# A two-layer encoder trunk on one core: the last expert pair's down weights handed over and loaded by column blocks

## The chip, the core and the metric

The kernel runs on one core of a Trainium2 chip. The metric is the device time of the kernel in microseconds (us). A run of another kernel is compared with runs of this one on the same chip.

## The reference, cut to what matters

The trunk has two layers for 256 tokens of width 2048, in float32. Layer 0 mixes tokens with a chunkwise mLSTM, layer 1 with latent attention (MLA). Behind each mixer stands a mixture of experts: 16 experts of inner width 512, two for each token.

```python
def moe_ffn(xn, router_w, router_b, w_gate, w_up, w_down):
    ...
    gates = jnp.sum(jax.nn.one_hot(eidx, N_EXPERTS, dtype=jnp.float32) * w[..., None], axis=1)
    hg = jnp.einsum('td,edf->tef', xt, w_gate)
    hu = jnp.einsum('td,edf->tef', xt, w_up)
    a = jax.nn.silu(hg) * hu * gates[..., None].astype(xt.dtype)
    y = jnp.einsum('tef,efd->td', a, w_down)
```

One expert has three matrices of 4 MB: gate and up (2048 x 512) and down (512 x 2048). So a layer's experts are 192 MB, of which each weight is used once.

## The kernel before

**Units and pairs.** The weights come in units of 1 MB: 128 partitions by 4 contraction steps by 512 columns for gate and up; for down, 128 partitions by one contraction step by all 2048 columns (kept as four blocks of 512). Two experts form a pair and are multiplied side by side, each in one half of TensorE's output partitions. A pair has 24 units, numbered n = 0 to 23: for each half q of the gates and ups the units 8q to 8q + 3 (gate) and 8q + 4 to 8q + 7 (up), then 16 to 23 (down). Eight pairs make the layer: k = 0 to 191 within a layer. The last pair is k = 168 to 191, and its down units are k = 184 to 191.

**Places.** A unit is loaded into one of 18 (and a few more) places in SBUF, two to a double buffer: 0 to 7 are the ring that the mixers also use, 8 and 9 lie in AREA, 10 and 11 over HI, 12 and 13 over the first half of XT_BOTH, 14 and 15 over its second half, 16 and 17 in SPARE. The function seat (L118) says which place a unit gets; for nearly all of a layer it goes round in steps of 18. Before the change the last pair's units 176 to 183 (second half of gates and ups) lie in places 10 to 17, after 158 to 165, and 184 to 191 in places 0 to 7, after 166 to 173.

**Who loads.** All weights go through SP's queue in an order written out by hand (experts, L550). Before a load, SP waits in room (L554) until the unit that held the place is consumed; TensorE counts consumed units in the semaphore unit_used, by the last matmul of each unit (finished, L1159). SP's queue is in order: what waits holds everything behind it. Most of a layer is loaded two units at a time, 2 MB in rows of 16 KB; the last pair is loaded unit by unit, 1 MB in rows of 8 KB (L618 to L621), units 181 and 183 in two halves each with rows of 4 KB (L622 to L629).

**The last four units.** Units 188 to 191 are the second half of the contraction of the pair's down matrices (for both experts). They are not loaded as units but as eight DMAs of 512 KB by column blocks d = 0 to 3, two for each block (L630 to L635). Each takes, for two contraction steps, 512 columns: rows of 2 KB. Both DMAs of a block count on one semaphore, and the function by_columns (L146) gives these places two turns.

**The pair on TensorE.** pair (L1156) multiplies gates and ups into banks 0 and 1 (L1183), scatters the pair before in between, turns the activation (L1203) and its selection (L1206, L1208), and multiplies with the down weights into banks 4 to 7. A float32 matmul is two records in the profile. For a normal pair, and for the first two of the four contraction steps c of the last pair, the loop is over c outside and over the column blocks d inside (L1226). For c = 2 and 3 of the last pair the loop over d is outside: it waits for the two DMAs of block d, does 8 matmul records (L1239), tells ScalarE that the block is done, and scatters block d - 1 (L1126, L1127). In layer 0, turn_final (L1062), which turns the first finished columns for the next mixer, stands between the last block's matmuls and the scatter of block 2. Then comes scatter_last (L1130).

**Behind a block.** ScalarE copies and rounds block d (Y_hi, L1660), VectorE makes the low part (Y_lo, L2272), TensorE scatters both to tokens, and VectorE adds them to X (add_block, L2254). The additions of blocks 0 and 1 stand after the low parts of blocks 1 and 2, those of blocks 2 and 3 after the low part of block 3. In layer 1 the blocks of X are stored as they are final (L713, L716 and one store on ScalarE's queue).

**Behind layer 0.** The MLA mixer's weights come through the ring, places 0 to 7; each load waits for the last expert unit that held its place (unit, L510). ScalarE makes the high part of each unit (high, L1463), VectorE the low part (L1842). The turned tokens get their high part from ScalarE (final_high, L1632) and their low part from GpSimd (L742). TensorE multiplies in three passes (L804): high weights by high tokens, low weights by high tokens, and, for the first units last, high weights by low tokens.

Of the kernel before, what the change touches and what calls it, by code (L numbers as in the profile page):

```python
# [18 lines left out]
P = 128  # L19
# [5 lines left out]
UNIT_K = 4  # L25
# [70 lines left out]
BY_COLUMNS = PAIRS * PAIR_UNITS - 4  # L96
# [16 lines left out]
def in_turn(k):  # L113

    return k // 4 * 4 + (0, 2, 1, 3)[k % 4]


def seat(k):  # L118


    if k == ALONE:
        return WIDE + ONCE
    if k == WIDE + ONCE:
        return ALONE
    if EARLY <= k < EARLY + ALONE:
        return k - EARLY
    return k if k < WIDE - 2 else k + 2 if k < WIDE else k - 2 if k < WIDE + 2 else k if k < EARLY else (k - ONCE) % WIDE
# [7 lines left out]
def expert(u):  # L135

    return U_MOE0 <= u < U_CKV or u >= U_MOE1


def split(u):  # L140

    k, singles = (u - U_MOE0, SINGLES[0]) if u < U_CKV else (u - U_MOE1, SINGLES[1])
    return expert(u) and (k in singles or PAIRS * PAIR_UNITS - HALVES <= k < BY_COLUMNS)


def by_columns(u):  # L146

    return expert(u) and (u - U_MOE0 if u < U_CKV else u - U_MOE1) >= BY_COLUMNS


def places():

    slots, turns, held = [], [], [0] * EARLY

    for u in range(U_ALL):
        if u < U_MOE0:
            s = u % RING
        elif u < U_CKV:
            s = seat(u - U_MOE0)
        elif u < U_MOE1:  # L160
            s = (u - U_CKV) % RING
        else:
            k = seat(u - U_MOE1)
            s = (k + U_MOE1 - U_CKV) % RING if k < RING else k
        if by_columns(u):
            held[s] += 2
        elif not expert(u) or s % 2 == 0 or split(u):
            held[s] += 1
        slots.append(s)
        turns.append(held[s])  # L170
    return slots, turns
# [67 lines left out]
def trunk(nc, w, out):  # L239
# [8 lines left out]
    with ctx:  # L248
# [258 lines left out]
        def _(sp):  # L507
# [42 lines left out]
            def experts(layer, base):  # L550
# [67 lines left out]
                for k in sorted(range(PAIRS * PAIR_UNITS - HALVES, BY_COLUMNS), key=in_turn):  # L618
                    room(k, 1)
                    if k - front not in LAST_UPS:  # L620
# [9 lines left out]
                room(BY_COLUMNS, 4)  # L630
                for d in range(4):
                    for k in (BY_COLUMNS, BY_COLUMNS + 2):
                        sp.dma_start(DOUBLE[PLACE[base + k]][:, :, d, :],
                                     all_of[k // 2].rearrange("p (k b c) -> p k b c", k=2, b=4)[:, :, d, :])\
                            .then_inc(sem(f"unit_loaded_{PLACE[base + BY_COLUMNS + d]}"), 16)  # L635

# [133 lines left out]
        def _(pe):  # L770
# [296 lines left out]
            def experts(l, base):  # L1067
# [88 lines left out]
                def pair(m, j, g, following, arrived, slot, consumed, whole, prev, first=False, opened=False, late=False):  # L1156
# [60 lines left out]
                    last_one = whole and not following  # L1217
                    for c in range(FC // 2 if last_one else FC):
# [15 lines left out]
                    for d in range(4 if last_one else 0):  # L1234
                        unit_arrived(pe, base + BY_COLUMNS + d)
                        for c in range(FC // 2, FC):
                            for e in range(2):
                                n = 16 + 4 * (c // 2) + 2 * e + c % 2
                                last = pe.matmul(PS[64 * e:64 * e + 64, 4 + d, :], m_["AT"][:, c, 64 * e:64 * e + 64],  # L1239
                                                 slot(n)[:, d, :], start=False, stop=(c == FC - 1))  # L1240
                                if d == 3:
                                    finished(last, n)
                        if d < 3:
                            last.then_inc(sem(m + "y_done"), 1)
                        if d == 3 and l == 0:
                            turn_final(0)
                        if d:
                            scatter(m, j, d - 1, True)
# [1341 lines left out]

# [13 lines left out]
```

## Time and profile before

| | us |
|---|---|
| median of 3 runs | 1668.2 (1666.77 to 1669.68) |
| the profiled execution | 1667.65 |
| its span, first to last instruction | 1665.6 |
| TensorE busy with matmuls | 1613.5 (97%) |
| VectorE busy | 763.7 (46%) |
| ScalarE busy | 481.3 (29%) |
| bytes moved by the DMA engines | 533.74 MB, mean 320 GB/s |

Times of an event are counted from the span's start. A row of the timeline has the start, the duration, the engine, the line of the kernel, the operation, what it writes and reads, and how many like it were merged; in square brackets the idle time ahead of it and what ended it. Matmuls are pipelined, so the duration of one is longer than the step from it to the next. A row of SP's queue is the issue of a DMA, not its transfer.

### The profile page before, as it was taken

Reading aid. Unit: us, or ns where it says so; the run is one execution under the profiler, and the core shown is the slowest. Engines: PE = TensorE matmul, PEld = TensorE weight load, DVE = VectorE, ACT = ScalarE, POOL = GpSimd, SP = SyncE. Lnnn points to the kernel's source line nnn. Section 1 sums busy time; section 2 is a strip of 40 time slices with the busy share of each in tenths; the row PEclk is TensorE's granted clock in tenths of the full one; section 3 lists DMA queues with packets and bytes.
Section 4 is the critical chain, followed back from the end, with each engine's and each line's share of the span. In section 5 each row is a group of like instructions: output and inputs, shape, how many; then the busy total and the mean of one; then the engine's idle time right before and its main releaser. Section 6 shows DMA issues by size and latency. Waiting matters only on the chain.

```text
span 1665.6 us, 19483 instructions
## 1 busy us (share of the span) xinstructions
PE 1613.5 (97%) x8047; PEld 1013.9 (61%) x8047; DVE 763.7 (46%) x1310; ACT 481.3 (29%) x620; POOL 54.1 (3%) x32
## 2 busy tenths in 40 slices
PE   9999999999999999988999999999999999989997
PEld 7888888887433434333359999888753344334343
DVE  6885477754332222212257777784532323222222
ACT  6445456443100000000054566564320000000000
POOL 3000000000000000000030000020000000000000
PEclk9999999999999999999999999999999999999999
DMA  8765656477999999999995545554799999999998
GB/s 293 266 201 161 200 153 220 151 257 303 422 415 421 429 427 427 428 427 426 420 352 174 159 139 151 197 178 152 287 422 421 424 428 428 427 428 428 429 420 327
DMA packets 117809, 533.74 MB, mean 320 GB/s; under 512 B 13108, under 2 KB 32088, under 8 KB 86488
## 3 DMA queue, kind: packets, MB, share of 16 engines
q1 hardware_dynamic: 117200, 532.06, 81.8%
q8 instruction: 66, 1.08, 0.3%
q10 hardware_dynamic: 488, 0.40, 0.1%
q14 instruction: 23, 0.19, 0.0%
q0 software_dynamic: 32, 0.02, 0.0%
HBM read 530.33 MB, written 2.11 MB: 320 GB/s over the span
## 4 chain that ended last, share of the span: by engine, by line
PE 81%; DMA 15%; DVE 1%; SPq 1%; ACT 1%; issue 0%; DVEq 0%; ACTq 0%
PE PS L804 33%; PE PS L1183 21%; PE PS L1226 8%; DMA DOUBLE<-in_moe_w_down 4%; DMA SPARE<-in_moe_w_gate 4%; DMA OVD<-in_moe_w_gate 3%; PE PS L915 3%; DMA OVD<-in_moe_w_down 2%; PE PS L1089 2%; DMA WIDED<-in_moe_w_gate 2%; PE PS L1126 2%; PE PS L936 1%; PE PS L921 1%; PE PS L1127 1%; PE PS L1109 1%; PE PS L1014 1%
## 5 line engine op out<-in xcount | busy, mean ns | idle before, releaser
L1842 DVE TENSOR_TENSOR LO<-ring,HI 128x2048 fp32r<-128x2048 f32 (+1 forms) x124 | 267.1, 2154 | 164.1 <-ACT HI L1463 163.5
L1183 PE MATMUL PS<-DOUBLE,AREA 128*64 128x512 f32 x1136 | 309.3, 598 | 8.8 <-DMA OVD<-in_moe_w_gate 5.4
L1463 ACT ACTIVATE HI<-ring 128x2048 fp32r<-128x2048 f32 (+1 forms) x124 | 223.6, 1803 | 260.4 <-PE PS L804 233.8
L804 PE MATMUL PS<-HI,XT_BOTH 128*128 128x512 f32 (+1 forms) x1344 | 297.9, 373 | 0.6 <-issue 0.6
L804 PEld LDWEIGHTS PS<-HI,XT_BOTH 128*128 128x128 f32 x1344 | 243.9, 188 | 35.0 <-issue 1.9
L1183 PE MATMUL PS<-OVD,AREA 128*64 128x512 f32 x464 | 209.5, 602 | 3.5 <-DMA SPARE<-in_moe_w_up 2.7
L1183 PEld LDWEIGHTS PS<-DOUBLE,AREA 128*64 128x64 f32 x1136 | 98.1, 139 | 177.8 <-issue 177.5
L1226 PE MATMUL PS<-DOUBLE,AREA 128*64 128x512 f32 x592 | 156.3, 595 | 8.0 <-DMA DOUBLE<-in_moe_w_down 7.6
L2264 DVE TENSOR_TENSOR AREA<-PS,VFF 128x512 f32<-128x512 f32 x64 | 44.1, 689 | 238.1 <-PE PS L1089 204.8
L804 PE MATMUL PS<-LO,XT_BOTH 128*128 128x512 f32 (+1 forms) x672 | 152.5, 368 | 0.0
L1650 ACT ACTIVATE AREA<-PS 128x512 f32<-128x512 f32 x16 | 9.6, 597 | 439.4 <-PE PS L1183 439.4
L804 PEld LDWEIGHTS PS<-LO,XT_BOTH 128*128 128x128 f32 x672 | 122.9, 188 | 16.2
L2254 DVE TENSOR_TENSOR X<-PS,X 128x512 f32<-128x512 f32 x112 | 69.9, 682 | 121.2 <-PE PS L1127 121.2
L1660 ACT ACTIVATE Y_hi<-PS,AREA 128x512 fp32r<-128x512 f32 x64 | 44.0, 687 | 230.2 <-PE PS L1226 195.3
L1183 PEld LDWEIGHTS PS<-OVD,AREA 128*64 128x64 f32 x464 | 63.0, 140 | 65.0 <-issue 65.0
L1226 PEld LDWEIGHTS PS<-DOUBLE,AREA 128*64 128x64 f32 x592 | 50.3, 137 | 81.8 <-issue 77.1
L2272 DVE SCALAR_TENSOR_TENSOR Y_lo<-PS,AREA,Y_hi 128x512 fp32r<-128x512 f32 x64 | 48.0, 751 | 107.9 <-ACT Y_hi L1660 103.1
L1183 PE MATMUL PS<-SPARE,AREA 128*64 128x512 f32 x208 | 92.5, 594 | 0.0
L1183 PE MATMUL PS<-WIDED,AREA 128*64 128x512 f32 x192 | 86.8, 596 | 0.0
L1089 PEld LDWEIGHTS PS<-AREA,XN 128*128 128x128 f32 x448 | 47.9, 140 | 34.0 <-issue 34.0
L1226 PE MATMUL PS<-OVD,AREA 128*64 128x512 f32 x144 | 63.9, 595 | 3.4 <-DMA WIDED<-in_moe_w_down 3.4
L1089 PE MATMUL PS<-AREA,XN 128*128 128x128 f32 x448 | 61.2, 280 | 0.0
(331 smaller groups left out, 1843.8 us busy)
## 6 DMA issues: line engine op xcount, KB each, us to landing
DOUBLE<-in_moe_w_up SPq DMA_DIRECT2D x26, 2048.0 KB, 24.4
ring<-in_a_w_in SPq DMA_DIRECT2D x48, 1024.0 KB, 5.2
DOUBLE<-in_moe_w_gate SPq DMA_DIRECT2D x24, 2048.0 KB, 21.4
DOUBLE<-in_moe_w_down SPq DMA_DIRECT2D x24, 2048.0 KB, 28.6
DOUBLE<-in_moe_w_down SPq DMA_DIRECT2D x26, 1024.0 KB, 9.0
ring<-in_b_w_in SPq DMA_DIRECT2D x32, 768.0 KB, 4.5
DOUBLE<-in_moe_w_gate SPq DMA_DIRECT2D x22, 1024.0 KB, 11.5
DOUBLE<-in_moe_w_up SPq DMA_DIRECT2D x20, 1024.0 KB, 14.0
```

The lines of the kernel that those rows point to most:

```text
L804: mm = pe.matmul(PS[:, banks[t], 0:n], lhs(k0 + kk, t)[part], weights[:, kk, 0:n], start=first and kk == 0 and p == 0, stop=last and kk == ...
L915: pe.matmul(PS[:, 4 * (b % 2) + ch, :], HI[u % 2][:, kk, ch * P:(ch + 1) * P], XT_BOTH[:, :, k, :], start=k == 0, stop=False)
L1089: last = pe.transpose(PS[:, GATHER_BANKS[g] + k // 2, at_:at_ + P], XN[:, t, c * P:(c + 1) * P], m_["SEL"][:, t, :])
L1126: pe.matmul(PS[:, bank, :], SCT[:, t * P:(t + 1) * P], YH[:, d, :], start=True, stop=False)
L1183: last = pe.matmul(PS[64 * e:64 * e + 64, up, :], tokens_of(c, e), slot(units[e])[:, kk, :], start=(c == 0), stop=(c == DC - 1))
L1226: last = pe.matmul(PS[64 * e:64 * e + 64, 4 + d, :], m_["AT"][:, c, 64 * e:64 * e + 64], slot(units[e])[:, d, :], start=(c == 0), stop=(c ...
L1463: act.activation(HI[s % 2][:, :, 0:n], ring[PLACE[u]][:, :, 0:n], ACT.Copy).then_inc(sem("hi_ready"), 1)
L1660: act.activation(YH[:, d, :], PS[:, 4 + d, :], ACT.Copy, scale=m_["GS"])\
L1842: tt(LO[PLACE[u]][:, :, 0:n], ring[PLACE[u]][:, :, 0:n], HI[s % 2][:, :, 0:n], ALU.subtract)\
L2254: tt(xs, PS[:, bank, :], xs, ALU.add).then_inc(sem(counted), 1)
L2264: tt(m_["XG"][:, 4 * g:4 * g + 4, :].rearrange("p k (t s) -> p k t s", t=NT), PS[:, banks[g]:banks[g] + 2, :].rearrange("p b (k t s) -> p ...
L2272: stt(YL[:, d, :], PS[:, 4 + d, :], m_["GS"], YH[:, d, :], ALU.mult, ALU.subtract)\
```

## The change

The host hands over one more input, last_down, which holds the down matrices of each layer's last pair again, cut as [layer, expert, block d, 128 partitions, 4 contraction steps x 512 columns]. Each of the eight down units 184 to 191 of the last pair is now one such piece: unit 184 + 2d + e is block d of expert e with all four contraction steps, 1 MB that is contiguous in memory, in rows of 8 KB, loaded by one DMA with a semaphore and a turn of its own. by_columns and its double turns are gone.

The places of the last pair's second half are exchanged: 176 to 183 go to places 0 to 7, and 184 to 191 to places 10 to 17. Units from 184 on are consumed in the order of their numbers (in_turn).

On TensorE the last pair's down matmuls are all done by blocks in a new function: for each d it waits for both units, does the four contraction steps (16 matmul records), and scatters block d - 1 after the second of them.

```diff
-BY_COLUMNS = PAIRS * PAIR_UNITS - 4
+BY_COLUMNS = PAIRS * PAIR_UNITS - 8
@@ def in_turn(k):
-    return k // 4 * 4 + (0, 2, 1, 3)[k % 4]
+    return k if k >= BY_COLUMNS else k // 4 * 4 + (0, 2, 1, 3)[k % 4]
@@ def seat(k):
+    if k >= BY_COLUMNS:
+        return k - BY_COLUMNS + RING + 2
+    if k >= BY_COLUMNS - RING:
+        return k - BY_COLUMNS + RING
@@ experts, on SP
-                for k in sorted(range(PAIRS * PAIR_UNITS - HALVES, BY_COLUMNS), key=in_turn):
+                for k in sorted(range(PAIRS * PAIR_UNITS - HALVES, PAIRS * PAIR_UNITS), key=in_turn):
                     room(k, 1)
-                    if k - front not in LAST_UPS:
+                    if k >= BY_COLUMNS:
+                        d, e = divmod(k - BY_COLUMNS, 2)
+                        sp.dma_start(in_double(base + k).rearrange("p k c -> p (k c)"), w["last_down"][layer, e, d])\
+                            .then_inc(sem(f"unit_loaded_{PLACE[base + k]}"), 16)
+                    elif k - front not in LAST_UPS:
...
-                room(BY_COLUMNS, 4)
-                for d in range(4):
-                    for k in (BY_COLUMNS, BY_COLUMNS + 2):
-                        sp.dma_start(DOUBLE[PLACE[base + k]][:, :, d, :],
-                                     all_of[k // 2].rearrange("p (k b c) -> p k b c", k=2, b=4)[:, :, d, :])\
-                            .then_inc(sem(f"unit_loaded_{PLACE[base + BY_COLUMNS + d]}"), 16)
@@ pair, on TensorE
-                    last_one = whole and not following
-                    for c in range(FC // 2 if last_one else FC):
+                    if whole and not following:
+                        down_by_columns(m, j, slot, finished)
+                        return
+                    for c in range(FC):
...
+                def down_by_columns(m, j, slot, finished):
+                    for d in range(4):
+                        for e in range(2):
+                            unit_arrived(pe, base + BY_COLUMNS + 2 * d + e)
+                        if d == 2:
+                            pe.wait_ge(sem(m + "sct_ready"), j + 1)
+                        for c in range(FC):
                             for e in range(2):
-                                n = 16 + 4 * (c // 2) + 2 * e + c % 2
+                                n = BY_COLUMNS - (PAIRS - 1) * PAIR_UNITS + 2 * d + e
                                 last = pe.matmul(PS[64 * e:64 * e + 64, 4 + d, :], m_["AT"][:, c, 64 * e:64 * e + 64],
-                                                 slot(n)[:, d, :], start=False, stop=(c == FC - 1))
-                                if d == 3:
+                                                 slot(n)[:, c, :], start=(c == 0), stop=(c == FC - 1))
+                                if d and c == e == 0:
+                                    finished(last, n - 1)
+                                if c == FC - 1 and (e == 0 or d == 3):
                                     finished(last, n)
+                            if c == 1 and d:
+                                scatter(m, j, d - 1, True)
                         if d < 3:
                             last.then_inc(sem(m + "y_done"), 1)
                         if d == 3 and l == 0:
                             turn_final(0)
-                        if d:
-                            scatter(m, j, d - 1, True)
@@ on the host
+def down_blocks(inputs):
+    import numpy as np
+    pair = [PER_GRP * (2 + e) + PER_GRP - 1 for e in range(2)]
+    a = np.asarray(inputs["moe_w_down"])[:, pair].reshape(2, 2, 2, P, 2, 4, UNIT_C)
+    return np.ascontiguousarray(a.transpose(0, 1, 5, 3, 2, 4, 6).reshape(2, 2, 4, P, UNIT_K * UNIT_C))
```

## Rows read from the trace of the kernel before

**Rows 1.** The page: busy time, granted clock in 40 slices, issues with us to landing.

```profile
PE 1613.5 (97%) x8047; PEld 1013.9 (61%) x8047; DVE 763.7 (46%) x1310; ACT 481.3 (29%) x620; POOL 54.1 (3%) x32
...
PEclk9999999999999999999999999999999999999999
...
ring<-in_a_w_in SPq DMA_DIRECT2D x48, 1024.0 KB, 5.2
```

**Rows 2.** Windows: from:to, length, then the columns that the first row names.

```profile
core 0: us, PE busy (x) PEld busy (x) DVE busy (x) ACT busy (x) POOL busy (x), PEclk, DMA share, GB/s
...
881.00:1100.00 219.00, 219.00 (x1235) 203.64 (x1234) 158.50 (x317) 125.80 (x187) 0.00 (x0) 1.00 0.52 164
...
1614.00:1624.00 10.00, 9.85 (x46) 3.82 (x45) 3.40 (x6) 0.00 (x0) 0.00 (x0) 1.00 1.01 419
...
1644.00:1650.00 6.00, 5.00 (x26) 1.78 (x23) 0.30 (x1) 0.69 (x1) 0.00 (x0) 1.00 1.04 382
```

**Rows 3.** Timeline of SP's queue in layer 1: units 176, 184 to 187, the columns.

```profile
1587.50 4.31 SPq L563 DMA_DIRECT2D OVD<-in_moe_w_gate  x1
...
1613.88 10.43 SPq L563 DMA_DIRECT2D DOUBLE<-in_moe_w_down  x4
1624.35 19.84 SPq L633 DMA_DIRECT2D DOUBLE<-in_moe_w_down  x8
```

**Rows 4.** Timeline of TensorE: matmuls of units 173 and 175, of 180 and 182.

```profile
1615.14 3.66 PE L1183 MATMUL PS<-DOUBLE,AREA 128*64 128x512 f32 x16
...
1628.50 0.62 PE L1183 MATMUL PS<-OVD,AREA 128*64 128x512 f32 x1 [1.33 <-DMA SPARE<-in_moe_w_up]
```

**Rows 5.** Timeline of TensorE: layer 1's last pair, down matmuls.

```profile
1638.58 3.65 PE L1226 MATMUL PS<-DOUBLE,AREA 128*64 128x512 f32 x16 [0.75 <-DMA DOUBLE<-in_moe_w_down]
1643.57 3.65 PE L1226 MATMUL PS<-DOUBLE,AREA 128*64 128x512 f32 x16 [1.33 <-DMA DOUBLE<-in_moe_w_down]
...
1649.94 1.94 PE L1239 MATMUL PS<-DOUBLE,AREA 128*64 128x512 f32 x8 [1.00 <-DMA DOUBLE<-in_moe_w_down]
...
1655.92 1.94 PE L1239 MATMUL PS<-DOUBLE,AREA 128*64 128x512 f32 x8
```

**Rows 6.** Timeline of SP's queue: unit 187 and the last column DMA, both layers.

```profile
818.17 2.13 SPq L563 DMA_DIRECT2D DOUBLE<-in_moe_w_down  x1
...
839.45 1.82 SPq L633 DMA_DIRECT2D DOUBLE<-in_moe_w_down  x1
...
1622.19 2.12 SPq L563 DMA_DIRECT2D DOUBLE<-in_moe_w_down  x1
...
1643.01 1.19 SPq L633 DMA_DIRECT2D DOUBLE<-in_moe_w_down  x1
```

**Rows 7.** DMA issues of 1613.88, 1622.19, 1643.01, 818.17, 839.45: KB, us to landing.

```profile
DOUBLE<-in_moe_w_down SPq DMA_DIRECT2D x1, 1024.0 KB, 22.1
...
DOUBLE<-in_moe_w_down SPq DMA_DIRECT2D x1, 1024.0 KB, 21.2
...
DOUBLE<-in_moe_w_down SPq DMA_DIRECT2D x1, 512.0 KB, 12.1
...
DOUBLE<-in_moe_w_down SPq DMA_DIRECT2D x1, 1024.0 KB, 21.9
...
DOUBLE<-in_moe_w_down SPq DMA_DIRECT2D x1, 512.0 KB, 12.0
```

**Rows 8.** Timeline of TensorE in layer 0: last block, first unit's third pass.

```profile
852.03 1.94 PE L1239 MATMUL PS<-DOUBLE,AREA 128*64 128x512 f32 x8
...
861.43 2.07 PE L804 MATMUL PS<-HI,XT_BOTH 128*128 128x512 f32 x8
```

**Rows 9.** Timelines of ScalarE and GpSimd in layer 0, behind the last block.

```profile
854.04 0.69 ACT L1660 ACTIVATE Y_hi<-PS,AREA 128x512 fp32r<-128x512 f32 x1 [2.33 <-PE PS L1239]
...
856.43 1.14 ACT L1632 ACTIVATE XT_BOTH<-AREA 128x512 fp32r<-128x512 f32 x2
...
857.13 8.95 POOL L742 TENSOR_TENSOR XT_BOTH<-AREA,XT_BOTH 128x512 fp32r<-128x512 f32 x4 [518.26 <-ACT XT_BOTH L1632]
```

More of the change, by code:

```diff
@@ L142, in split @@
     k, singles = (u - U_MOE0, SINGLES[0]) if u < U_CKV else (u - U_MOE1, SINGLES[1])
-    return expert(u) and (k in singles or PAIRS * PAIR_UNITS - HALVES <= k < BY_COLUMNS)
-def by_columns(u):
-    return expert(u) and (u - U_MOE0 if u < U_CKV else u - U_MOE1) >= BY_COLUMNS
+    return expert(u) and (k in singles or k >= PAIRS * PAIR_UNITS - HALVES)
 def places():
@@ L164, in places @@
             s = (k + U_MOE1 - U_CKV) % RING if k < RING else k
-        if by_columns(u):
-            held[s] += 2
-        elif not expert(u) or s % 2 == 0 or split(u):
+        if not expert(u) or s % 2 == 0 or split(u):
             held[s] += 1
@@ L1233, in pair @@
                             gather(m, following, (1,))
-                    for d in range(4 if last_one else 0):
-                        unit_arrived(pe, base + BY_COLUMNS + d)
-                        for c in range(FC // 2, FC):
+                def down_by_columns(m, j, slot, finished):
[5 more added lines that the diff above has]
+                        for c in range(FC):
                             for e in range(2):
-                                n = 16 + 4 * (c // 2) + 2 * e + c % 2
+                                n = BY_COLUMNS - (PAIRS - 1) * PAIR_UNITS + 2 * d + e
                                 last = pe.matmul(PS[64 * e:64 * e + 64, 4 + d, :], m_["AT"][:, c, 64 * e:64 * e + 64],
-                                                 slot(n)[:, d, :], start=False, stop=(c == FC - 1))
-                                if d == 3:
+                                                 slot(n)[:, c, :], start=(c == 0), stop=(c == FC - 1))
+                                if d and c == e == 0:
+                                    finished(last, n - 1)
+                                if c == FC - 1 and (e == 0 or d == 3):
                                     finished(last, n)
+                            if c == 1 and d:
+                                scatter(m, j, d - 1, True)
                         if d < 3:
@@ L2598 @@
     arrays["in_consts"] = constants()
+    arrays["in_last_down"] = down_blocks(inputs)
     w = {n[3:]: nc.dram_tensor(n, a.shape, mybir.dt.float32, kind="ExternalInput").ap() for n, a in arrays.items()}
```

## The prediction

> **What bounds the kernel now.** I read the page first. TensorE is busy for 97% of the span and its granted clock stays in the top tenth, the 2.4 GHz level, throughout [rows 1]. The busy share alone does not say who sets the end, so I went stage by stage with the table of windows. In the latent-attention mixer, from 881 to 1100 us, TensorE is busy for all 219 us while the DMA engines are half idle: TensorE is the bound. In the experts, 1614 to 1624 us, the DMA engines are full at 419 GB/s [rows 2], and TensorE waits for weights again and again [rows 4, 5]: the load stream is the bound. The change touches both places where these stages meet something else: the end of layer 0's experts, where TensorE takes over, and the end of layer 1's, which is the end of the kernel. So I then read the timeline of SP's queue, TensorE's timeline around the last pair, and the issues with their time to landing. I price three things: when the last down weights land, how much TensorE has to do after that, and whether the new buffer order starves the stream.
>
> **When the weights land.** Units 184 to 187 are 1 MB in rows of 8 KB per partition. In layer 1 the first is issued at 1613.88 [rows 3] and lands 22.1 us later, at 1635.98; the fourth is issued at 1622.19 [rows 6] and lands 21.2 us later, at 1643.39 [rows 7]: 7.41 us for three, 2.47 us a unit. The window's 419 GB/s gives 1.049 MB / 419 GB/s = 2.50 us [rows 2]. I take 2.49. The eight column DMAs of 512 KB that follow read rows of 2 KB. The last is issued at 1643.01 [rows 6] and lands 12.1 us later, at 1655.1 [rows 7]: 11.7 us for 4 MB, 2.93 us per MB, and the stretch shows 382 GB/s [rows 2]. After the change these 4 MB are four more units with 8 KB rows: 1643.4 + 4 x 2.49 = 1653.35, so the last landing moves 1.75 us forward. Layer 0 in the same way: 818.17 + 21.9 = 840.07 [rows 6, 7]; the last column DMA lands at 839.45 + 12.0 = 851.45 [rows 6, 7]; after, 840.07 + 9.96 = 850.0, 1.4 us forward.
>
> **What TensorE does after the last landing.** Before, a block d needs only the second half of the contraction, 8 matmul records, and then scatters the block before it. From the first step after a wait, 1649.94, to the start of the last block, 1655.92, there are two such steps [rows 5], so one is 2.99 us; the last 8 records take 1.94 us and end at 1657.86 [rows 5]. TensorE is already 0.8 us behind the last landing there. After, a block holds all four contraction steps: 16 records and, between them, the scatter of the block before: 2.99 + 1.94 = 4.93 us. Blocks 0 and 1 use exactly the four units that arrived first before as well. Block 0 starts at 1638.58 as before and takes 3.65 us, block 1 waits until 1643.57 as before [rows 5]. Then the DMA's 2 x 2.49 = 4.98 us a block is just over TensorE's 4.93: block 2 starts near 1648.5, and block 3 waits for 1653.35 + 0.1 (the usual 0.05 to 0.15 from landing to start, 1643.39 to 1643.57 in these rows) = 1653.45 and ends at 1658.4. Against 1657.86 that is **+0.5 us**. The 1.75 us that the stream wins are spent because the last block carries 16 records and a scatter behind its landing, not 8. What follows, the copy, the low part, the additions of blocks 2 and 3 and the stores, has the same order on ScalarE and VectorE, so I carry it over unchanged. Moving scatter 2 ahead of the end saves nothing there: it lay beside ScalarE's 0.7 us copy and VectorE's low part anyway.
> Bounds: if all weights were there in time, TensorE alone would need two blocks without a gap, where the second 8 records cost 3.65 - 1.94 = 1.71 us [rows 5], and a last one: 1643.57 + 2 x 4.70 + 4.93 = 1657.9, so not below +0.05. From above, a stream at the 382 GB/s of its last stretch would land the last unit at 1643.4 + 4 x 2.74 = 1654.4 and end at 1659.4, +1.5.
>
> **Layer 0.** The last block ends at 852.03 + 1.94 = 853.97 now [rows 8]. After: 850.0 + 0.1 + 4.93 = 855.05, which is +1.1. Here scatter 2 comes before this end, and before it stood after it, so TensorE by itself would be back to about +0.1. But who waits for that end is ScalarE: its copy starts at 854.04, right behind; then the high part of the first mixer unit, the high part of the turned tokens at 856.43, and then GpSimd's low parts from 857.13, 2.24 us each (four in 8.95) [rows 9], two of them until 861.6. TensorE's third pass over the first unit starts at 861.43 [rows 8], at that very moment: this chain has no slack. It moves by the full **+1.1 us**, TensorE idles in front of it, and from there TensorE is the bound without a gap [rows 2], so nothing gives it back and layer 1 starts later by the same amount. Bounds: +0.1 if that chain has slack that I don't see, and +2.1 at 2.74 us a unit.
>
> **Waits and buffers.** The change swaps places. Units 176 to 183, the last pair's second gates and ups, now take the places of 166 to 173 instead of 158 to 165, so SP must wait longer before it issues them, and everything behind waits with it in SP's queue, the down units too. Now 176 is issued at 1587.50 [rows 3]. After, the last of them, 183, waits for unit 173, whose matmuls run from 1615.14 to 1618.8 [rows 4]. The stream doesn't feel this as long as it has work: TensorE waits for 182 until 1628.5 [rows 4], so at 1618.8 the engines still hold almost 10 us of loads. The 12 DMAs behind (four halves, eight down units) go out at 2.6 us each if SP is as slow as in its 10.43 us for four [rows 3]: the last by 1650.1, and the engines need it at 1650.9. I cost the longer wait at nothing; its cover is those 10 us of queued loads. The down units themselves wait for 158 to 165, free long before. The other side of the swap: places 0 to 7 are free earlier at layer 0's end, so the mixer's units 4 to 7 can be issued earlier. Nobody waits for them: TensorE has no gap on a DMA there [rows 2]. Instruction counts stay: the same matmuls, one more semaphore wait a block, eight issues for eight.
>
> **A rule weighed.** The rows say that row length matters here: 2.93 us per MB with rows of 2 KB, 2.49 with 8 KB [rows 2, 3, 6, 7]. The Trainium skill (DMA: Bandwidth & Descriptors, Specifications) puts the minimum for line rate at 512 B, by which 2 KB rows would be at line rate already and the last landing would stay where it is; this trace does not agree, and what would follow is my second rival. The same page (Anatomy of one DMA) fits a DMA as 2.0 us plus its bytes at 436 GB/s; taken one after another, eight of 512 KB would need 25.6 us and four of 1 MB 17.6. The rows have 11.7 us for the eight, so behind a filled queue the fixed part is hidden.
>
> **Sum.** +1.1 and +0.5 make +1.6 us. The profiled execution took 1667.65 us with a span of 1665.6; after, 1669.25. The three runs' median is 1668.2, 0.55 above the profiled one, so I predict 1669.8.
>
> **The rivals.**
> *The landing decides (faster).* If the last blocks followed the landing with the same delay as now, the 1.4 and 1.75 us would come through: 1668.2 - 3.15 = 1665.05. For it: TensorE does wait for DMAs up to 1649.94. Against: from there to the end it doesn't, and the last block gets twice its matmuls. Chance 0.07.
> *No earlier landing (slower).* The last unit lands at 851.45 and 1655.1 as before, be it that row length isn't what slows the last stretch but the end of the stream itself. Then 851.5 + 4.93 = 856.4 (+2.45) and 1655.15 + 4.93 = 1660.1 (+2.2): 1672.85. Against: it would have to come from the end of the stream, yet layer 0 has more loads queued behind and needs 11.4 us for its 4 MB too. Chance 0.10.
> *The stream runs dry (slower).* Place: SP's wait for unit 173. It decides once TensorE releases 173 less than an issue-to-landing time before the queue is empty; the 1 MB loads of the first mixer, with a short queue, take 5.2 us [rows 1], so from about 1623 on, 4 us later than I compute. It could come sooner if a thin queue runs slower. Price: each us dry is a us, in each layer; with 3 us each, 1669.8 + 6 = 1675.8. Chance 0.08.
> *Another placement of the tensors in memory*, now 16.8 MB more, changes the rate of all loads by a tenth of a per cent or two either way: no row prices it. Chance 0.05.
>
> **How the numbers follow.** The forecast has 0.70: +0.2 to +3.6 by the bounds above, so 1668.4 to 1671.8, and with the runs' scatter of 1.5 either way 1667 to 1673. The range 1666.8 to 1673.2 takes in the second rival too and leaves out the first and the third. A kernel like this can be told from no change by about 0.2%, 3.3 us. Faster by more: half of the first rival and some of the last, 0.06. Slower by more: the second and third, and the forecast's upper edge, 0.20. Within: 0.74.
>
> **What would show it.** Right: the down units of the last pair land 2.5 us apart up to about 1653.4 (plus layer 0's shift of 1.1); TensorE's blocks of 16 records start at their landings; the last block ends some 5 us after the last landing; in layer 0 a new idle gap of about 0.9 us before the mixer's first matmuls. Wrong: a DMA rate below 400 GB/s between 1618 and 1650, a TensorE wait for an up unit longer than now, landings 2.9 us apart, or a block that takes much more than 4.9 us.

## The result, and the profile after

The kernel before took 1668.2 us (median of 13 runs), the changed one 1672.3 us (13 runs, 1670.0 to 1673.1). The ratio is 1.0022, 95% interval 1.0015 to 1.0029, so the change costs 3.7 us (2.5 to 4.8); the two medians are 4.1 us apart. The forecast was 1669.8 within 1666.8 to 1673.2: the range and the sign are right, the size is 2.5 us short (+1.6 forecast, +4.1 by the medians). The profiled execution of the changed kernel took 1672.57 us.

The page first. TensorE's busy time is 0.2 us from that of [rows 1], its instructions are as many, and its clock is at the same level. TensorE does the same work and waits 5 us longer.

```profile
span 1670.6 us, 19479 instructions
...
PE 1613.7 (97%) x8047; PEld 1014.0 (61%) x8047; DVE 763.5 (46%) x1310; ACT 481.1 (29%) x620; POOL 54.1 (3%) x32
...
PEclk9999999999999999999999999999999999999999
```

The windows of the changed kernel answer to [rows 2]. The columns are from:to, length, then as the first row names them.

```profile
core 0: us, PE busy (x) PEld busy (x) DVE busy (x) ACT busy (x) POOL busy (x), PEclk, DMA share, GB/s
1616.00:1626.00 10.00, 10.00 (x46) 4.13 (x43) 2.48 (x4) 0.00 (x0) 0.00 (x0) 1.00 1.01 421
1626.00:1636.00 10.00, 8.50 (x39) 3.27 (x39) 1.98 (x3) 0.60 (x1) 0.00 (x0) 1.00 1.02 415
1646.00:1652.00 6.00, 4.93 (x20) 1.73 (x20) 0.75 (x1) 0.40 (x2) 0.00 (x0) 1.00 1.00 414
...
881.00:1100.00 219.00, 219.00 (x1228) 203.09 (x1227) 158.74 (x318) 124.02 (x184) 0.00 (x0) 1.00 0.52 165
```

The stretch near the end, 382 GB/s in [rows 2], is at 414 now, so the longer rows do load faster. The mixer, 881 to 1100, is as full as it was.

SP's queue in layer 1 answers to [rows 3] and [rows 6]. A row is the start, the time that the issues took, the line, and what is written from what. L628 are the halves of units 181 and 183, L619 the new down units.

```profile
1600.69 10.59 SPq L560 DMA_DIRECT2D DOUBLE<-in_moe_w_gate  x4
...
1622.16 1.75 SPq L628 DMA_DIRECT2D DOUBLE<-in_moe_w_up  x4
1623.96 0.91 SPq L619 DMA_DIRECT2D OVD<-in_last_down  x2
1624.91 2.09 SPq L619 DMA_DIRECT2D WIDED<-in_last_down  x2
1627.05 2.60 SPq L619 DMA_DIRECT2D OVD<-in_last_down  x2
1629.69 3.40 SPq L619 DMA_DIRECT2D SPARE<-in_last_down  x2
```

Unit 176 goes out at 1600.69, where [rows 3] have 1587.50. That is the longer wait for places. The twelve issues behind it take 10.9 us in all.

TensorE in layer 0, the changed kernel's timeline, answers to [rows 8]. L1241 are the down matmuls, L1120 a scatter's first matmul, L770 turn_final, L798 the mixer's matmuls (L804 before).

```profile
837.14 3.65 PE L1241 MATMUL PS<-OVD,AREA 128*64 128x512 f32 x16 [0.70 <-DMA OVD<-in_last_down]
842.11 1.94 PE L1241 MATMUL PS<-WIDED,AREA 128*64 128x512 f32 x8 [1.32 <-DMA WIDED<-in_last_down]
...
852.04 1.94 PE L1241 MATMUL PS<-SPARE,AREA 128*64 128x512 f32 x8
853.91 0.50 PE L1120 MATMUL PS<-Y_hi,SCT 128*128 128x512 f32 x1
...
855.05 1.94 PE L1241 MATMUL PS<-SPARE,AREA 128*64 128x512 f32 x8
856.92 1.09 PE L770 MATMUL PS<-CON,X 128*128 128x128 f32 x8
...
860.73 2.06 PE L798 MATMUL PS<-HI,XT_BOTH 128*128 128x512 f32 x8 [0.54 <-ACT XT_BOTH L1636]
...
864.44 2.09 PE L798 MATMUL PS<-HI,XT_BOTH 128*128 128x512 f32 x8
```

The last block ends at 855.05 + 1.94 = 856.99, 3.02 us later than in [rows 8], and the third pass starts at 864.44, 3.01 later. ScalarE and GpSimd, which answer to [rows 9], carry the same 3.02 us:

```profile
857.06 0.69 ACT L1664 ACTIVATE Y_hi<-PS,AREA 128x512 fp32r<-128x512 f32 x1 [4.35 <-PE PS L1241]
...
859.45 1.14 ACT L1636 ACTIVATE XT_BOTH<-AREA 128x512 fp32r<-128x512 f32 x2
```

```profile
860.15 8.94 POOL L736 TENSOR_TENSOR XT_BOTH<-AREA,XT_BOTH 128x512 fp32r<-128x512 f32 x4 [521.02 <-ACT XT_BOTH L1636]
```

TensorE in layer 1, the changed kernel's timeline, answers to [rows 5]:

```profile
1641.87 3.65 PE L1241 MATMUL PS<-OVD,AREA 128*64 128x512 f32 x16 [0.73 <-DMA OVD<-in_last_down]
1646.85 1.94 PE L1241 MATMUL PS<-WIDED,AREA 128*64 128x512 f32 x8 [1.32 <-DMA WIDED<-in_last_down]
...
1652.73 1.94 PE L1241 MATMUL PS<-OVD,AREA 128*64 128x512 f32 x8 [0.95 <-issue]
...
1657.72 1.94 PE L1241 MATMUL PS<-SPARE,AREA 128*64 128x512 f32 x8
...
1660.71 1.94 PE L1241 MATMUL PS<-SPARE,AREA 128*64 128x512 f32 x8
```

Block 2, due at once, waits 0.95 us. The timeline names "issue", yet the second of its two units landed at 1628.63 + 24.0 = 1652.6, by this row of the DMA issues (KB, us to landing):

```profile
OVD<-in_last_down SPq DMA_DIRECT2D x1, 1024.0 KB, 24.0
```

The eight units land at 1639.25, 1641.73, 1644.22, 1646.71, 1649.20, 1652.64, 1655.11 and 1657.58: 2.48 us apart but for one step of 3.44. In layer 0 all steps are 2.48 to 2.50, from 834.52 to 851.91.

### The profile page after: what moved, and what is told of

Its sections match the earlier page's. It is cut to its first block, busy times and chain, and to the rows that moved or that the text cites. A ratio compares the mean times of both kernels' runs of the same rounds, so it can differ in the third digit from the quotient of the medians.

```text
span 1670.6 us, 19479 instructions
## 1 busy us (share of the span) xinstructions
PE 1613.7 (97%) x8047; PEld 1014.0 (61%) x8047; DVE 763.5 (46%) x1310; ACT 481.1 (29%) x620; POOL 54.1 (3%) x32
## 4 chain that ended last, share of the span: by engine, by line
PE 81%; DMA 16%; DVE 2%; ACT 1%; issue 0%; SPq 0%; DVEq 0%; ACTq 0%
PE PS L798 33%; PE PS L1177 20%; PE PS L1222 8%; DMA DOUBLE<-in_moe_w_down 5%; DMA DOUBLE<-in_moe_w_gate 4%; DMA SPARE<-in_moe_w_gate 4%; PE PS L909 3%; DMA WIDED<-in_last_down 3%; PE PS L1083 2%; PE PS L1120 2%; PE PS L930 1%; PE PS L915 1%; PE PS L1241 1%; PE PS L1121 1%; PE PS L1103 1%; PE PS L1008 1%
## 5 line engine op out<-in xcount | busy, mean ns | idle before, releaser
L1177 PE MATMUL PS<-DOUBLE,AREA 128*64 128x512 f32 x1264 | 334.3, 595 | 10.6 <-DMA OVD<-in_moe_w_gate 5.4
L798 PE MATMUL PS<-HI,XT_BOTH 128*128 128x512 f32 (+1 forms) x1344 | 297.9, 373 | 1.1 <-issue 0.6
L798 PEld LDWEIGHTS PS<-HI,XT_BOTH 128*128 128x128 f32 x1344 | 243.9, 188 | 35.5 <-issue 2.4
L1177 PEld LDWEIGHTS PS<-DOUBLE,AREA 128*64 128x64 f32 x1264 | 107.2, 138 | 194.4 <-issue 194.1
L1177 PE MATMUL PS<-OVD,AREA 128*64 128x512 f32 x400 | 177.7, 595 | 0.4 <-DMA SPARE<-in_moe_w_up 0.4
L798 PE MATMUL PS<-LO,XT_BOTH 128*128 128x512 f32 (+1 forms) x672 | 152.5, 368 | 0.0
L1222 PE MATMUL PS<-DOUBLE,AREA 128*64 128x512 f32 x528 | 141.7, 595 | 4.2 <-DMA DOUBLE<-in_moe_w_down 3.8
L798 PEld LDWEIGHTS PS<-LO,XT_BOTH 128*128 128x128 f32 x672 | 122.9, 188 | 16.2
L1222 PEld LDWEIGHTS PS<-DOUBLE,AREA 128*64 128x64 f32 x528 | 45.7, 137 | 69.5 <-issue 66.2
L1177 PEld LDWEIGHTS PS<-OVD,AREA 128*64 128x64 f32 x400 | 53.8, 138 | 44.4 <-issue 44.4
L1177 PE MATMUL PS<-SPARE,AREA 128*64 128x512 f32 x176 | 78.5, 594 | 1.0 <-DMA DOUBLE<-in_moe_w_gate 1.0
L1177 PE MATMUL PS<-WIDED,AREA 128*64 128x512 f32 x160 | 72.2, 596 | 1.6 <-DMA OVD<-in_moe_w_up 1.6
L1222 PE MATMUL PS<-OVD,AREA 128*64 128x512 f32 x144 | 63.9, 595 | 3.4 <-DMA WIDED<-in_moe_w_down 3.4
```

Of the source, the lines that this page charges most:

```text
L798: mm = pe.matmul(PS[:, banks[t], 0:n], lhs(k0 + kk, t)[part], weights[:, kk, 0:n], start=first and kk == 0 and p == 0, stop=last and kk == ...
L1177: last = pe.matmul(PS[64 * e:64 * e + 64, up, :], tokens_of(c, e), slot(units[e])[:, kk, :], start=(c == 0), stop=(c == DC - 1))
```

## The experiments

Theory A, that of the prediction: the last landing comes forward, but the last block now has 16 matmul records and a scatter behind its landing, and this costs more. Rival B: the second copy of the weights in memory, or its place, is what costs. Rival C: the exchange of places costs, through SP's later issues. Rival D: rows of 8 KB bring nothing. Beside them stood the question which part of the last block could be spared.

The table cuts each profiled execution at the same events: the landing of unit 187 (the fourth down unit), the end of the last down block on TensorE, and the span's end. All are us. The last column is the median beside the kernel before on the same chip, as a ratio with its 95% interval.

| kernel | 187 lands, layer 0 | to block end | to landing, layer 1 | to block end | to span end | ratio |
|---|---|---|---|---|---|---|
| before | 840.09 | 13.88 | 789.46 | 14.43 | 7.7 | |
| changed | 841.97 | 15.02 | 789.72 | 15.94 | 7.9 | 1.0022 [1.0015, 1.0029] |
| changed, again | 842.76 | 15.11 | 789.97 | 15.73 | 7.9 | 1.0020 [1.0011, 1.0029] |
| places as before | 841.82 | 15.02 | 789.90 | 15.72 | 7.9 | 1.0018 [1.0009, 1.0027] |
| scatter 2 behind | 841.70 | 13.72 | 789.56 | 14.94 | 7.7 | 1.0010 [1.0001, 1.0019] |
| half blocks, 8 KB | 840.03 | 13.23 | 789.34 | 14.22 | 7.7 | 0.9997 [0.9988, 1.0006] |
| handed over only | 840.52 | 13.41 | 790.39 | 13.36 | 7.9 | 1.0002 [0.9993, 1.0011] |
| whole blocks, 2 KB | 842.74 | 16.10 | 790.66 | 16.45 | 7.9 | 1.0035 [1.0021, 1.0049] |
| before, longer start | 849.52 | 13.35 | 791.00 | 13.29 | 7.9 | 1.0063 [1.0049, 1.0077] |
| changed, longer start | 850.77 | 15.03 | 790.60 | 14.82 | 7.9 | 1.0075 [1.0061, 1.0088] |

Columns two to five hold what the change does near its place; the first holds what an execution had gathered before it reached the changed part.

**Handed over only.** The kernel before, with the last pair's down weights read from a second tensor of the same size as the change's, in the same rows and the same order.

```diff
-                        single(base + k, all_of[k // 2])
+                        single(base + k, all_of[k // 2] if k < BY_COLUMNS - 4 else w["last_down"][layer, k // 2 % 2, 0])
...
-                                     all_of[k // 2].rearrange("p (k b c) -> p k b c", k=2, b=4)[:, :, d, :])\
+                                     w["last_down"][layer, k // 2 % 2, 1].rearrange("p (k b c) -> p k b c", k=2, b=4)[:, :, d, :])\
```

> The kernel before, with one thing changed: the last pair's down matrices come from a second tensor of 16.8 MB that the host hands over, cut as before (the same row lengths, the same DMAs, the same order). In the two profiles the changed kernel is 1.9 us later than before already at unit 187 of layer 0, ahead of everything that the change touches on TensorE. Theory A (that offset is the scatter of single executions, and the change costs where TensorE and the stream meet): no difference, -0.8 to +0.8 us against the kernel before. Rival B (the extra tensor places the weights differently in memory and the loads run slower): +1.5 to +2.5 us, and the landings drift apart in the expert stages.

Measured: 1667.54 us against 1668.22. Rival B falls: another 16.8 MB in memory and reading from it cost nothing that can be told (by the interval at most 1.8 us). (In the table its 13.36 is short and its 790.39 long because unit 187 itself was late, 3.09 us after the one before.)

**Scatter 2 behind the last block.** The changed kernel; the scatter of block 2 no longer stands in the middle of block 3 but behind it.

```diff
-                            if c == 1 and d:
+                            if c == 1 and d in (1, 2):
                                 scatter(m, j, d - 1, True)
...
                             turn_final(0)
+                        if d == 3:
+                            scatter(m, j, 2, True)
```

> The changed kernel, but the scatter of block 2 stands behind the last block's matmuls (in layer 0 behind turn_final too), as in the kernel before, not in their middle. Theory A (what sets the end is the chain that begins when the last block's matmuls end: ScalarE's copy and what hangs on it, in both layers): the last block ends 1.0 us earlier behind the same landing, in layer 0 and in layer 1, so 2.0 us less than the changed kernel, or +1.5 to +2.5 us against the kernel before. My prediction said that this scatter's place saves nothing in layer 1 (it costs nothing beside ScalarE's copy), without seeing that it costs its 1.0 us where it stands now. Rival B (placement) and rival C (the exchange of places starves the stream): no difference to the changed kernel, about +4.1 us against the kernel before.

Measured: 1669.18 us, 3.2 us below the changed kernel's 1672.33 (2.0 us by their two ratios), and 1.0 us above the kernel before. TensorE's timeline of this kernel in layer 0:

```profile
851.77 3.65 PE L1241 MATMUL PS<-SPARE,AREA 128*64 128x512 f32 x16
855.36 1.09 PE L770 MATMUL PS<-CON,X 128*128 128x128 f32 x8
856.21 0.47 PE L1120 MATMUL PS<-Y_hi,SCT 128*128 128x512 f32 x1
...
859.14 2.06 PE L798 MATMUL PS<-HI,XT_BOTH 128*128 128x512 f32 x8
```

and in layer 1:

```profile
1651.30 1.94 PE L1241 MATMUL PS<-OVD,AREA 128*64 128x512 f32 x8 [1.23 <-issue]
...
1656.27 3.65 PE L1241 MATMUL PS<-SPARE,AREA 128*64 128x512 f32 x16
```

The last block is one row of 16 records of 3.65 us, not 4.93 in three pieces. From the landing of 187 to its end is 1.3 us less in layer 0 and 1.0 less in layer 1, and the mixer's first matmuls (859.14) have no gap before them. The scatter itself then fills time in which TensorE would have waited for ScalarE: from the block's end to the mixer's first row are 859.14 - 855.42 = 3.72 us with it and 860.73 - 856.99 = 3.74 without it. So over half of what the change costs is this one scatter, standing where ScalarE's chain waits for the block.

**Half blocks in 8 KB rows.** The kernel before; only contraction steps 2 and 3 are handed over, four units of 1 MB with block d of both experts, in rows of 8 KB. Steps 0 and 1, the last block of 8 records and the scatter behind it stay.

```diff
-                for k in sorted(range(PAIRS * PAIR_UNITS - HALVES, BY_COLUMNS), key=in_turn):
+                for k in sorted(range(PAIRS * PAIR_UNITS - HALVES, PAIRS * PAIR_UNITS), key=in_turn):
                     room(k, 1)
+                    if k >= BY_COLUMNS:
+                        sp.dma_start(in_double(base + k).rearrange("p k c -> p (k c)"), w["last_down"][layer, k - BY_COLUMNS])\
...
-                                n = 16 + 4 * (c // 2) + 2 * e + c % 2
                                 last = pe.matmul(PS[64 * e:64 * e + 64, 4 + d, :], m_["AT"][:, c, 64 * e:64 * e + 64],
-                                                 slot(n)[:, d, :], start=False, stop=(c == FC - 1))
+                                                 slot(20 + d)[:, 2 * e + c % 2, :], start=False, stop=(c == FC - 1))
```

> The kernel before with only the row length changed: units 184 to 187 and all of TensorE's order as before, but the second half of the contraction is handed over as four units of 1 MB, one for each column block d with both experts and both contraction steps, in rows of 8 KB, one DMA each in place of two with rows of 2 KB. Places as before. Theory A: the last landing comes 1.7 us earlier, but TensorE, which needs 3.46 us for c = 1 and then 1.9 + 3.0 + 3.0 + 1.9 us, has the end from the landing of unit 187 on: the last block ends 1.0 us earlier in layer 1 (its wait of 1.0 us goes) and 0.4 us earlier in layer 0, together -1.4 us against the kernel before (-0.5 to -2.5). Rival B: the same gain less 1.5 to 2 us for placement, so about +0.3. Rival D (row length isn't what slowed the stream's end): 2 KB or 8 KB, the landings stay 2.7 to 2.9 us per MB apart, and no difference.

Measured: 1667.69 us, not to be told from the kernel before; the profiled execution is 1.1 us shorter in its span. The last landing is early, 850.03 where the kernel before has 851.41, and still the block's end gains only 0.65 us in layer 0 and 0.2 in layer 1. Beside the handed-over kernel, whose landings behind unit 187 are even, it gains 0.2 in layer 0 too (13.23 against 13.41). TensorE's timeline of this kernel in layer 0 says why:

```profile
840.16 3.65 PE L1216 MATMUL PS<-DOUBLE,AREA 128*64 128x512 f32 x16 [1.31 <-DMA DOUBLE<-in_moe_w_down]
843.62 3.63 PE L1228 MATMUL PS<-DOUBLE,AREA 128*64 128x512 f32 x16
847.18 0.50 PE L1116 MATMUL PS<-Y_hi,SCT 128*128 128x512 f32 x1
...
851.32 1.94 PE L1228 MATMUL PS<-DOUBLE,AREA 128*64 128x512 f32 x8
```

After its last wait at 840.16 TensorE has no gap to 853.26. From there TensorE, not the landing, is the bound, and 13.2 us is what its work takes in this order. In layer 1 it does wait once:

```profile
1648.90 1.94 PE L1228 MATMUL PS<-DOUBLE,AREA 128*64 128x512 f32 x8 [0.80 <-DMA DOUBLE<-in_last_down]
```

This is a late landing of the changed kernel's kind: 1645.10, then 1648.86, 3.76 us apart.

**Places as before.** The changed kernel with the old order of places.

```diff
-    if k >= BY_COLUMNS:
-        return k - BY_COLUMNS + RING + 2
-    if k >= BY_COLUMNS - RING:
-        return k - BY_COLUMNS + RING
```

> The changed kernel without the exchange of places: units 176 to 183 again in places 10 to 17 behind 158 to 165, the down units 184 to 191 in places 0 to 7 behind 166 to 173. Theory A: SP issues units 176 to 183 some 13 us earlier and nothing else moves, because the engines had 10 us of loads queued all the time: no difference to the changed kernel, about +4.1 us against the kernel before (+3.3 to +4.9). Rival C (the later issue costs, by a thinner queue or by SP's waits): 1 us or more less than the changed kernel.

Measured: 1671.59 us, ratio 1.0018 beside 1.0022 and 1.0020 of the changed kernel, so the same. SP's queue in layer 1 issues the halves up to 15 us earlier than the changed kernel:

```profile
1606.93 2.08 SPq L624 DMA_DIRECT2D OVD<-in_moe_w_up  x1
...
1617.79 15.36 SPq L615 DMA_DIRECT2D DOUBLE<-in_last_down  x8
```

and the fourth down unit lands at 1646.74, in the changed kernel at 1646.71. Rival C falls: the stream was full either way.

**Changed, again.** The changed kernel unaltered, for a second profile and a second median.

> The changed kernel itself, once more. Theory A and every rival: about +4 us against the kernel before (+3 to +5). Its profile is read for two things that one execution can't tell: whether the 1.5 us that the loads are behind before the changed part begins are there again, and whether the step of 3.4 us in place of 2.5 between two landings of layer 1's down units is there again, beside a fetch of 16 KB of instructions.

Measured: 1671.33 us. The table's columns two to five agree with the first profile within 0.25 us each. The late landing is there again at the same unit (1650.34 to 1653.73, 3.39 us), and block 2 waits 0.91 us. The loads are late ahead of the changed part again, but in another way: 2.5 us already at the first expert load, which lands at 265 us in the kernel before, and 2.7 us at the landing of 822 us.

**The same blocks in rows of 2 KB.** The changed kernel; each down unit is read from the original matrices by two DMAs of 512 KB.

```diff
-                        sp.dma_start(in_double(base + k).rearrange("p k c -> p (k c)"), w["last_down"][layer, e, d])\
-                            .then_inc(sem(f"unit_loaded_{PLACE[base + k]}"), 16)
+                        for c in range(2):
+                            sp.dma_start(in_double(base + k)[:, 2 * c:2 * c + 2, :],
+                                         all_of[(BY_COLUMNS + 4 * c + 2 * e) // 2].rearrange("p (k b c) -> p k b c", k=2, b=4)[:, :, d, :])\
+                                .then_inc(sem(f"unit_loaded_{PLACE[base + k]}"), 16)
```

> The changed kernel with the row length put back: the same units, places, order and matmuls, but each down unit is loaded from the original down matrices by two DMAs of 512 KB in rows of 2 KB. Theory A (row length sets how far apart they land: 2.73 us per MB by the 382 GB/s of the column DMAs, against 2.49): unit 187 lands 1.0 us later and the last 1.9 us later than in the changed kernel; 5.46 us a block is then longer than TensorE's 4.93, so the last block ends 1.9 us later in each layer: +3.8 us against the changed kernel, about +7.8 us against the kernel before. Rival D (row length doesn't matter, the end of the stream was slow for another reason): no difference to the changed kernel, about +4 us.

Measured: 1673.82 us, ratio 1.0035 [1.0021, 1.0049], so 2.5 us above the changed kernel beside it. The sign is right, the size smaller than the 3.8 us expected. Windows of this kernel, with the columns as above:

```profile
1634.00:1644.00 10.00, 8.90 (x44) 3.96 (x40) 2.90 (x6) 0.60 (x1) 0.00 (x0) 1.00 1.04 392
1644.00:1654.00 10.00, 8.02 (x36) 2.99 (x36) 0.75 (x1) 0.69 (x1) 0.00 (x0) 1.00 1.05 387
```

and TensorE's last block in layer 1:

```profile
1661.02 1.94 PE L1245 MATMUL PS<-SPARE,AREA 128*64 128x512 f32 x8 [1.09 <-DMA SPARE<-in_moe_w_down]
...
1664.01 1.94 PE L1245 MATMUL PS<-SPARE,AREA 128*64 128x512 f32 x8
```

The whole of 8 MB goes at 387 to 392 GB/s; every other DMA lands 2.7 us after the one before (in layer 1 1647.31, 1650.01, 1652.73, 1655.43, 1658.02). That is 0.2 us more for each MB than with 8 KB rows, as expected (2.73 against 2.49). Rival D falls too, and in layer 1 last block and landing now stand as Theory A says: 1660.88 lands, 1661.02 starts, 1665.95 ends, 4.93 us. The DMAs are also half as large here, but size isn't it: the 512 KB halves of units 181 and 183, in rows of 4 KB, land 1.27 us apart in the changed kernel (1634.22, 1635.48, 1636.75), 2.5 us for each MB. The short rows also lie apart in memory, where the handed-over pieces are contiguous; these two weren't separated.

Why the median moved by 2.5 us and not 3.8 isn't shown. In the profiles the local cost is larger: from the last landing ahead of the down units to the end of the last block are 28.40 and 27.30 us, in the changed kernel 24.96 and 25.90. In layer 1 there is no late landing here, which saves 1 us. In layer 0 there is one, unit 187 at 842.74, 4.16 us after the unit before it. TensorE idles 3.23 us for it, and behind this wait the granted clock is 0.57 between 843 and 847 us, so mostly at the 1.2 GHz level: the first 8 records take 3.20 us and not 1.94. The timeline's row, and the window with its columns as above:

```profile
842.88 3.20 PE L1245 MATMUL PS<-WIDED,AREA 128*64 128x512 f32 x8 [3.23 <-DMA WIDED<-in_moe_w_down]
```

```profile
843.00:847.00 4.00, 4.00 (x11) 1.44 (x11) 0.00 (x0) 0.00 (x0) 0.00 (x0) 0.57 1.06 389
```

This execution was also the slowest of its five (1675.82).

**Both kernels with a longer start.** An attempt to move the instruction fetches against the stream: 32 small matmuls at the start in place of two wide ones, once in the kernel before, once in the changed one.

```diff
-            fill(512, 512)
+            fill(*(32 for _ in range(32)))
```

> The kernel before, with 120 instructions more on TensorE in its first 5 us: its two filling matmuls of 512 columns are 32 of 32 columns, which take about as long and compute nothing that is used. So each fetch of 16 KB of TensorE's instructions behind comes at another point of the work, by roughly half a block. Theory E (a fetch holds one DMA engine for 1.1 us, and the stream loses that where it comes at a bad moment; where it comes is an accident of the program's length): the time moves by 0.5 to 2 us either way against the kernel before, and the landing that is late in layer 1 (1649.9) is another one or none. Rival F (the fetches cost the same wherever they are): -0.5 to +0.5 us, and the same landings.

> The changed kernel with the same 120 instructions more at the start. Theory E: the offset of 1.5 us ahead of the changed part and the late landing in layer 1 (0.95 us) are accidents of where the fetches come; one or both go or change, and the time moves by up to 2.5 us, rather down than up, to between +1.5 and +4.5 us against the kernel before. Rival G (both belong to the change): +3.5 to +4.5 us as the changed kernel.

Measured: 1678.06 and 1680.96 us, both some 10 us above what they should be. Neither range expected against the kernel before holds, and as a test of the fetches this was a poor one. The row of the small matmuls, in the kernel before so altered, where the two wide ones took 3.78 us:

```profile
1.59 13.87 PE L869 MATMUL PS<-AREA 128*128 128x32 f32 x64 [1.59 <-DVE AREA L1831]
```

What it does give: with all of the kernel later by the same 10 us, the changed kernel is still 2.9 us slower than the one before (1679.4 to 1681.2 against 1677.1 to 1678.9). And in the changed kernel the late landing has moved from unit 189 to unit 187 (1652.92 to 1656.40, 3.48 us), where TensorE waits 2.32 us for it and not the usual 1.32:

```profile
1656.53 1.94 PE L1241 MATMUL PS<-WIDED,AREA 128*64 128x512 f32 x8 [2.32 <-DMA WIDED<-in_last_down]
...
1669.28 1.94 PE L1241 MATMUL PS<-SPARE,AREA 128*64 128x512 f32 x8
```

From that landing to the block's end are then 14.82 us, 0.15 below the 14.97 of the prediction, since no further landing is late. In the kernel before with the longer start it is unit 187 too that lands late (1650.03 to 1653.87, 3.84 us):

```profile
1654.00 3.65 PE L1226 MATMUL PS<-DOUBLE,AREA 128*64 128x512 f32 x16 [2.67 <-DMA DOUBLE<-in_moe_w_down]
...
1665.22 1.94 PE L1239 MATMUL PS<-DOUBLE,AREA 128*64 128x512 f32 x8
```

From it to the block's end are 13.29 us. So this pair compares the two orders behind even landings: +1.5 us in layer 1, and +1.7 in layer 0 (15.03 against 13.35).

## Why the prediction was right or wrong

**When the weights land: right in layer 0, one step off in layer 1.** From unit 187 to the last landing are 851.91 - 841.97 = 9.94 us in layer 0; the prediction had 4 x 2.49 = 9.96. In layer 1 it is 10.87.

**What TensorE does after it: right.** 16 records and a scatter take 4.95 us in layer 0 (852.04 to 856.99 with no gap) and 4.93 in layer 1, TensorE keeps up with two units of 2.49 and no more, and from a landing of 187 to the end of the last block layer 0 takes 15.02 us; the prediction had 855.05 - 840.07 = 14.98, that is +1.1.

**Layer 0's +1.1: right beside this profile, and passed on in full.** ScalarE's copy, the high part, GpSimd and the third pass are all 3.01 to 3.03 us later, the 1.9 us of the first column and these 1.1. The mixer gave nothing back (789.7 to layer 1's landing, against 789.5). The gap before the mixer's first matmuls is 0.54 us, where 0.9 was said. But the size is partly luck. In the profile of the kernel before, the first column is complete 3.19 us after unit 187 (840.09 to 843.28), and TensorE waits 0.44 us at 846.03. In the handed-over kernel that step is 2.71 us, TensorE doesn't wait, and the block ends after 13.41 us, not 13.88; with the longer start after 13.35. Against these the change costs 1.6 to 1.7 us in layer 0.

**Layer 1's +0.5: the term that was mis-sized.** It measured +1.5 (15.94 against 14.43), and +1.3 the second time. The failed step is "block 3 waits for 1653.35 + 0.1", which spaced the four landings evenly. One of them was 0.95 us late, and in the new order block 2 waits for it at once and all behind it has no slack: 0.5 + 0.95. The kernel before has a late landing too. Its four columns are complete 2.71 us apart in layer 0 (843.28, 845.99, 848.70, 851.41), but in layer 1 at 1646.13, 1649.90, 1652.50 and 1655.06, with one step of 3.77. I read its effect, the 1.00 us of idle at 1649.94 in [rows 5], as the stream's pace, and took 2.93 us for each MB as the mean over it. At 2.71 that column is complete at 1648.84, TensorE doesn't wait, and the kernel before ends its last block 1.0 us earlier. So I set an uneven stream before against an even one after; both with a late landing, as they ran, are 1.5 us apart, and so are the two with the longer start, even behind unit 187 (14.82 against 13.29).

**Scatter 2: rightly counted, wrongly judged.** The 4.93 us contained it, and the sum came out. But the sentence that moving it ahead "saves nothing there" looked only at where it had been. Where it went, it stands on the path of every block's end: the scatter behind the block takes 1.3 and 1.0 us back. Without it the change's local cost is -0.2 us in layer 0 and +0.5 in layer 1, beside the profile of the kernel before.

**Waits and buffers at nothing: right.** Places as before gives the same time. The pace of SP's queue was wrong in my working: 2.6 us an issue, the last at 1650.1. It issued the last at 1632.03, since after the long wait an issue took from 0.43 us and not 2.1. The cover was wider than I said. "Eight issues for eight" was a slip: the kernel before issues twelve DMAs for these units, the changed one eight.

**The rivals.** The landing that decides fell: with half blocks it comes 1.4 us earlier in layer 0, and the block's end gains 0.65 us. No earlier landing fell as well (9.94 us for the four units in layer 0, 11.32 before). The stream never ran dry, and the second tensor costs nothing that can be told; the size that the prediction gave to placement came from no row. The Trainium skill (DMA: Bandwidth & Descriptors, Specifications) would have rows of 2 KB at line rate; the experiment that reads the same units in rows of 2 KB has 387 to 392 GB/s for them against 414 to 421, and 2.5 us of the kernel's time. Here the measurement decides. The fit that the prediction took from the same page of the Trainium skill (Anatomy of one DMA) is for DMAs issued from GpSimd, and these are issued from SP; no term of the sum used it.

**The sum.** The local columns add to 1.1 + 0.3 + 1.5 + 0.2 = 3.1 us in the first profile and 3.2 in the second, inside the 2.5 to 4.8 us measured by the medians. The two profiled executions are 4.9 us apart because the changed one was 1.9 us late before it reached anything that the change touches. At the landing that comes at 822 us in the kernel before, the changed kernel is 2.0 us late, its second profile 2.7, places as before 1.8 and scatter 2 behind 0.8; the handed-over kernel is 0.4 us late, the whole blocks in rows of 2 KB 0.3, the half blocks not at all. The difference jumps at one or two steps of the stream, while TensorE's and SP's code up to there is the same. In the changed kernel it goes from -0.3 to +1.5 us at the landing of 495 us. This is not the scatter of one execution: the same landing is late by 1.0 to 1.3 us in the other three profiles of whole blocks in 8 KB rows with the usual start, by 0.2 with 2 KB rows, and not at all in the handed-over and half-block kernels. It comes again with the program, so the medians may hold some of it beside the 3.1 us. Its cause stays open. The range held because it had room for scatter and for a rival that didn't come, and not because the sum came out: the sum had 1.6 of the 3.1 us measured locally.

**The late landing.** Its cause stays open too. In layer 1 of most profiles an instruction fetch of 16 KB, 1.1 us long, begins 2.1 to 2.6 us before it (1650.35 for 1652.64, in the kernel before 1647.46 for 1649.90, with the longer start 1654.27 for 1656.40). But in layer 0 the same kind of fetch at 840.75 delays nothing, and in the handed-over kernel the fetch, at 1648.12, begins 3.8 us after the late landing of 1644.32. With 2 KB rows the landing 2.3 us after the fetch at 1658.58 is late by under 0.2 us. That the fetch is the cause wasn't shown.

## What to carry to other kernels

An earlier last landing is worth only what the consumer's work behind it leaves: count that work first, and keep the last piece small. With the full contraction and a scatter behind the last landing the 1.4 us won became 1.1 us lost in layer 0, and 1.3 us of that was the scatter. Work whose result is not needed yet doesn't belong between a landing and the operation that the next engine waits for; moved behind it, it was free, where in front it cost a microsecond in each layer. When a wait in the profile is read as a stream's pace, look at the landings before and after it: a single late one has to be set into both kernels or into neither.

## What was not expected of the hardware

The issue of a DMA of 1 MB took 2.12 us in the kernel before [rows 6], where SP never waited long for a place, and 0.33 to 0.43 us for the first ones in the changed kernel behind the longer wait (two of 1 MB in 0.91 us). With the places as before they took 2.1 us again. A float32 matmul of 128x32 isn't cheap for being narrow: 32 of them, two records each, take 13.87 us, 0.43 a call, where two of 512 columns take 3.78. Between 2 and 6 us the engine's weight loads are busy for all 4 us, 20 of them. And one late step in a stream of even landings, 3.1 to 3.8 us in place of 2.5 to 2.7, came at layer 1's end in nine of the ten profiles, also where nothing was changed; in the tenth, whole blocks in rows of 2 KB, layer 0 has one instead.
